# Two more units by half-size products, thinner filler in the mixer heads, and an exponential table loaded earlier

## What is computed

```python
h = rms_norm(x, norm_mix_pre[l])
z = h @ w_in[l]                      # 1024 -> 6144 columns
q_h, f_fw, f_bw, i_h, g_h, q_d, k_d, v_d, gate_a, gate_b = split(z)
a = hgrn2_mixer(q_h, f_fw, f_bw, i_h, g_h, ...)      # 4 heads of 128
b = diff_attention(q_d, k_d, v_d, ...)               # 4 heads, softmax over keys
m = sigmoid(gate_a) * (a @ w_branch_a[l]) + sigmoid(gate_b) * (b @ w_branch_b[l])
x = x + rms_norm(m @ w_out[l], norm_mix_post[l])
```

## Time and profile before

| | us |
|---|---|
| median of 3 runs | 2477.68 |
| lowest and highest | 2475.63, 2479.24 |
| the profiled execution | 2476.72 |
| its span | 2474.6 |

### The profile page before, as it was taken

How to read it: one execution, slowest core, us unless ns; L and a number is a source line. 1 busy time by engine, 2 the same in 40 slices (tenths; PEclk the granted TensorE clock), 3 DMA queues, 4 the chain that set the end, 5 groups by cost and what they waited for, 6 DMA issues and landing times.

```text
span 2474.6 us, 41229 instructions
## 1 busy us (share of the span) xinstructions
PE 2451.5 (99%) x16634; PEld 2262.0 (91%) x16634; DVE 1830.5 (74%) x2427; ACT 1280.8 (52%) x1962; POOL 187.0 (8%) x236
## 2 busy tenths in 40 slices
PE   9999999999999999999999999999999999999998
PEld 9999988898899999888899998898889999997887
DVE  6656777754788999978575567776548888999784
ACT  4444666543355555556444456665424555564563
POOL 0001011100200000003110011011002000000031
PEclk9999999999999999999999999999999999999999
DMA  5464444244323233833334544343543232347421
GB/s 171 124 185 134 142 131 144 86 173 168 103 71 88 75 100 112 306 102 137 96 119 129 173 147 137 119 137 108 185 145 97 70 94 81 94 148 261 149 99 60
DMA packets 290267, 321.53 MB, mean 130 GB/s; under 512 B 10400, under 2 KB 223904, under 8 KB 290080
## 3 DMA queue, kind: packets, MB, share of 16 engines
q1 hardware_dynamic: 215744, 171.39, 23.4%
q10 hardware_dynamic: 74336, 147.53, 16.9%
HBM read 253.60 MB, written 65.27 MB: 129 GB/s over the span
## 4 chain that ended last, share of the span: by engine, by line
PE 91%; DVE 3%; ACT 2%; issue 1%; DMA 1%; POOL 1%; SPq 0%; ACTq 0%; POOLq 0%; DVEq 0%
PE ps L851 21%; PE ps L1138 14%; PE ps L1319 13%; PE ps L1074 8%; PE ps L1057 5%; PE ps L809 5%; PE ps L1425 5%; PE ps L823 3%; PE ps L1259 2%; PE ps L1285 2%; PE ps L1027 2%; PE ps L1405 1%; PE ps L909 1%; PE ps L1046 1%; PE ps L1007 1%
## 5 line engine op out<-in xcount | busy, mean ns | idle before, releaser
L851 PE MATMUL ps<-hT_hi,whi 128*128 128x384 f32 x608 | 204.0, 336 | 1.0 <-ACT U L2956 0.6
L851 PE MATMUL ps<-hT_lo,whi 128*128 128x384 f32 x608 | 203.1, 334 | 0.0
L851 PE MATMUL ps<-hT_hi,wlo 128*128 128x384 f32 x608 | 203.1, 334 | 0.0
L2005 DVE TENSOR_TENSOR wlo<-raw,whi 128x1024 fp32r<-128x1024 f32 (+1 forms) x154 | 165.3, 1074 | 41.9 <-ACT whi L2941 41.9
L2956 ACT ACTIVATE U<-ps 128x384 f32<-128x384 f32 x152 | 74.8, 492 | 218.3 <-PE ps L851 218.3
L1319 PE MATMUL ps<-whi,PH_hi 128*128 128x512 f32 x456 | 179.1, 393 | 0.5 <-issue 0.5
L1319 PE MATMUL ps<-whi,PH_lo 128*128 128x512 f32 x456 | 177.7, 390 | 0.0
L1319 PE MATMUL ps<-wlo,PH_hi 128*128 128x512 f32 x456 | 177.6, 390 | 0.0
L1503 DVE TENSOR_TENSOR wlo<-raw,whi 128x2048 fp32r<-128x2048 f32 x53 | 122.2, 2306 | 69.2 <-ACT whi L2326 69.2
L1607 DVE TENSOR_TENSOR wlo<-raw,whi 128x1024 fp32r<-128x1024 f32 (+1 forms) x98 | 102.8, 1069 | 77.4 <-ACT whi L2483 77.3
L851 PE MATMUL ps<-S_hi,whi 128*128 128x384 f32 x456 | 152.5, 334 | 0.0
(11 more groups left out here) (316 smaller groups left out, 7039.8 us busy)
## 6 DMA issues: line engine op xcount, KB each, us to landing
raw<-w_up_dram SPq DMA_DIRECT2D x88, 512.0 KB
raw<-w_in_dram SPq DMA_DIRECT2D x64, 512.0 KB
raw<-w_down_dram SPq DMA_DIRECT2D x60, 512.0 KB, 4.9
raw<-w_in_dram SPq DMA_DIRECT2D x16, 1024.0 KB
zT<-gst ACTq DMA_DIRECT2D x40, 384.0 KB, 2.5
GT<-zT ACTq DMA_DIRECT2D x16, 768.0 KB, 5.9
pD<-CG ACTq DMA_DIRECT2D x26, 384.0 KB, 2.3
zT<-hn ACTq DMA_DIRECT2D x48, 192.0 KB, 2.1
```

What stands on the lines that cost most here:

```text
L851: ins = mm(ps[:, 4 * (j % 2) + bank, 0:TH], quarter(L, W[y], j, (w,))[:, 0, k * P:(k + 1) * P], sum_operand(a, x, k), start=(opens and k = ...
L2005: v.tensor_tensor(quarter(L, wlo, j, names), raw_quarter(j, names), quarter(L, whi, j, names).bitcast(F32), ALU.subtract)\
```

## The change

Two gate units, (None, 0) and (None, 4), move from the filler into the run of half-size products, so fourteen units of a layer are made so. The filler has seven units, 56 parts, and `SLOTS` gives each head 14 in place of 18. A one-column activation with Exp is put behind the squares of each head.

```diff
-IN_UNITS = [(0, TOKEN_U), (1, TOKEN_U)] + [(h, u) for h in range(NH) for u in range(3)] + [(2, TOKEN_U), (3, TOKEN_U)]\
-    + [(None, u) for u in range(2 * NH)]
+IN_UNITS = [(0, TOKEN_U), (1, TOKEN_U)] + [(h, u) for h in range(NH) for u in range(3)] + [(None, 0), (None, NH)]\
+    + [(2, TOKEN_U), (3, TOKEN_U)] + [(None, u) for u in range(2 * NH) if u % NH]
-I0, I1 = 2, 14
-DENSE = 15
+I0, I1 = 2, 16
+DENSE = 17
-SLOTS = ((0, 2, 2, 2, 2, 2, 2, 1, 1, 0, 1, 1, 2),) * (NH - 1) + ((0, 2, 2, 2, 2, 2, 2, 1, 1, 0, 1, 2, 1),)
+SLOTS = ((0, 2, 2, 1, 1, 2, 1, 1, 1, 0, 1, 1, 1), (0, 2, 2, 2, 1, 1, 2, 1, 1, 0, 1, 1, 0),
+         (0, 2, 2, 1, 1, 2, 1, 1, 1, 0, 1, 1, 1), (0, 2, 2, 2, 1, 1, 2, 1, 1, 0, 1, 0, 1))
...
+        exp_ahead = keep("exp_ahead", [P, 1])
...
-                    if h is None:
+                    if h is None and I0 <= j < I1:
+                        load(unit(L, j), [rows(w_in, L, 0, KD, 8 * HW + u * 256 + b * P, P) for b in range(2)])
+                    elif h is None:
                         load(unit(L, j), [rows(w_in, L, 0, KD, 8 * HW + u * 256, 256)])
...
+            def exponential_table(it):
+                if it:
+                    done(A_table, it - 1, "in")
+                a(exp_ahead[:], half_neg[:, 0:1], ACT.Exp).then_inc(*A_table.step("in"))
...
                 a(SQ1[:], view(ps[:], GB[0] * 512, [[P, NT], [1, P]]), ACT.Square).then_inc(*G_sq.step("sq"))
+                exponential_table(it)
                 side(TAIL + 2)
...
-                    unit_stored(L, N_IN - NH)
+                    unit_stored(L, head_unit(None, NH))
```

More of the change, by code:

```diff
@@ L433, in build @@
         A_pool = steps("att_pool", ["ms", "rs"])
+        A_table = steps("exponential_table", ["in"])
         ab_act = steps("ab_act", [f"h{c}" for c in range(KD)])
```

## The result

The changed kernel takes 2498.68 us, median of 4 runs (2498.09 to 2499.42), against 2478.46 for the kernel before in runs beside it: ratio 1.0078, 95% interval 1.0066 to 1.0089. It is slower, by 20 us, where 14 were forecast. The profiled execution is 2499.42 (span 2497.6), 22.7 above that of before.

What follows compares the result with a forecast made beforehand. PE was taken to bound both the half-size stage and the heads, where filler hides a chain. Per layer -4.5 + 15.1 - 2.6 - 0.7 = +7.3, both layers +14.6 on 2476.7: forecast 2491.5 us, range 2474 to 2500.

Steps and rivals of the forecast that it cites:

- the balance: Per layer, saved PE work of 4.5 us against 15.1 us of new waits in the heads, so slower.
- half-size stage: Stage ahead of the heads: two more units of half-size products add 28.9 us a layer in full.
- single slots: Six one-part slots in heads 1 to 3 wait 0.45 us each for the At copy, 2.7 a layer.
- token slots: Two head 0 slots, cut to one half tile of the token unit, wait 1.05 us each, 2.1 a layer.
- head 2's split: Weight split in head 2's one-part slot 4 makes the values of tile 4 wait 0.9 us.
- first border: Head 1 to 2, no filler left: waits of 1.3 us for tile 0's weighting and 1.1 for its values.
- second: Border of heads 2 and 3, one part kept but the split late: wait of 1.4 us.
- head 3's tail: Before head 3's last transposes, one of three parts is left: 3.4 us of bare wait.
- the table: Early exponential table load removes PE's waits for the output copy in the heads: -2.6 us a layer.
- head 0's tail: The split's low part, now in slot 7, delays DVE's row; PE waits 2.2 us.
- The rival: Head 3's bare wait drops the clock to 1.2 GHz, some 3 us a layer more, 2497 us; 8%.
- QK: Earlier weight load shortens DVE's wait for head 1's QK transfer: -0.7 us a layer, within 0 to 2.

Runs made afterwards that it cites:

- e3: Changed kernel with the weight split (high and low) of the filler's first gate unit moved from slot 7 to slot 8 of head 0: 2494.03 us, ratio 1.0065.
- e5: Changed kernel with two filler parts of head 3 moved from slots 3 and 6 to slot 11, ahead of the last transposes: 2492.31 us, ratio 1.0048.
- e11: Changed kernel with ACT's copy of the turned weights (At) placed before both exponentials of the next tile, not behind them: 2486.73 us, ratio 1.0024.
- e1: Changed kernel without the one-column Exp, so the table load stands at the first exponentials again: 2498.10 us, ratio 1.0083.
- e2: Kernel before (twelve units) with only the one-column Exp added behind the squares: 2470.77 us, ratio 0.9969.
- e10: Changed kernel with 11 and 14 unread matmuls in PE's waits before head 0's far products and head 3's last transposes: 2493.91 us, ratio 1.0052.
- e9: e2 with head 2's QK transfer issued ahead of the weight load it stood behind: 2469.57 us, ratio 0.9955.
- e6: Changed kernel with one filler part of head 1 moved from slot 6 to slot 12: 2498.87 us, ratio 1.0075.

## Why the prediction was right, and where it was off

**Right: the balance.** Work of -4.5 a layer against new waits of some 15 gave the sign. The half-size stage was +29.15 for +28.9. Filler moved as counted, and seven of the eight kinds of waits stand where they were put, within 0.25 us: single slots 0.45 (0.45), token slots 1.11 (1.05), head 2's split 0.95 (0.9), first border 1.33 and 1.24 (1.3 and 1.1), second 1.26 (1.4), head 3's tail 3.63 (3.4). Head 1 came out at -7.57 for -7.4. e3, e5 and e11 each took one of these waits away by taking away what made it.

**Right for another reason: the table.** -2.6 a layer was entered for it. e1 shows that in this kernel the column does nothing measurable; the waits went with the slots. Read as a step, it was wrong, and it hid that the column alone was worth having (e2).

**Mis-sized: head 0's tail**, 2.2 forecast. The wait, 2.63 from start to start (2.35 in layer 1), is near it, and e3 shows that it needs the low: without it 0.36 is left, though the rope still waits 1.69. But part of it is that wait of the rope for the QK transfer, which I had called harmless after looking at head 1 alone. The high that the low needs ended at 322.37 and the low began at 323.23, so up to some 0.8 us is the transfer's by these rows, an estimate; no run takes the transfer alone away. To that extent the wait came near 2.2 by luck. Then the clock fell behind it, which cost 1.3 and 0.7 us by e10, 1.4 and 1.2 by the rows at full clock. Head 0 was +0.10 and -0.36 for -1.95: the largest miss, 3.6 us over both layers.

**The clock had been priced in the wrong place.** The rival put it at head 3 alone, with 3 us a layer. It fell in head 0 in both layers, behind waits of 2.46 and 2.18, and in head 3 only in layer 1. Together it cost 3.2 us (e10) to 3.8, not 6, and its place was not among the rivals. This is the mechanism at little over half its size, beside the forecast and not in its stead.

**Not foreseen in head 3 and head 2**, 0.7 and 0.4 a layer: in slot 5 of head 3 the turning of weights waits 0.50 for an output copy that stands on ACT behind the split's high. No row names the rest.

**Outside the heads**, +2.8 in layer 0, -1.1 in layer 1 and -0.7 ahead of both. In layer 0's down projection one row answers for part:

```profile
1024.37 0.47 PE L1324 MATMUL ps<-whi,PH_hi 128*128 128x512 f32 x1 [1.00 <-DVE PH_lo L1900]
```

Over the kernels of this study the same stretch of layer 0 took 764.8 to 768.1 us with no edit in it, so I give this no cause. Adding up: 14.6 forecast, + 0.5 half-size stages, + 3.6 head 0, - 0.1 head 1, + 2.2 heads 2 and 3, + 1.3 behind head 3 in layer 1, + 1.0 outside, is 23.1, against 23.0 between the spans. The medians differ by 20.2; the profiled executions lie at the upper end of one kernel and the lower end of the other.

**QK**: -0.7 was entered within 0 to 2; on twelve units it is worth 1.0 to 1.4 (e9), in head 1 of the changed kernel DVE's wait for the transfer fell from 4.43 to 0.89, and what that brought PE is not measured by itself.

## What to carry to other kernels

Before filler is thinned, count the distance from each step's first dependent instruction to its last and compare it with the work that stays. Here 4.5 us of saved products a layer met 15 us of chain that the filler had hidden, and nearly half of what PE then waited (13.0 of some 29 us over both layers) was one copy queued behind two exponentials. Shorten the chain first (a copy placed ahead, a transfer sent ahead of a weight load, a table loaded where ACT is idle), see what releases a transfer (here the last scores) and how much work is left to cover it, and look up which part of a unit then stands in each slot, since moving one part moved a bank's copy-out into the way in two experiments. When a wait of PE is filled with unread products to test the clock, size them to end with the wait: 24 in place of 14 cost head 3 1.7 us a layer and hid the whole effect.

## What the runs showed of the hardware

The clock's fall does not follow from the length of one wait alone. Head 3's last turning waited 3.4 to 3.5 us in five of these kernels. In the changed kernel the clock stayed at 1.00 in layer 0 and went to 0.50 in layer 1; in e3 it was the other way round; in e6 it fell in layer 1 only; in e1 and e11 it fell in both. In head 0 it fell behind waits of 2.46 and 2.18 in the changed kernel. It did not in layer 0 of e6, where the far products took 1.99 us after a wait of 2.57, nor in layer 1 of e1 (2.35) and of e11 (2.56). e11's layer 0 after that turning:

```profile
516.00:520.00 4.00, 0.56 (x3) 0.26 (x2) 1.85 (x3) 1.16 (x2) 1.52 (x2) 0.84 1.03 416
520.00:524.00 4.00, 4.00 (x16) 4.00 (x16) 3.04 (x5) 1.99 (x3) 0.00 (x0) 0.50 0.21 84
```

Once it had fallen, it stayed at 0.50 for some 3 to 6 us with PE busy, and a fall cost 1.1 to 2.3 us. That idling lets it fall and work brings it back agrees with the Trainium skill (TensorE: Matmul & The Clock Gate, What's actually happening); why the same wait has two outcomes stays open.
